# Feed-forward weight splits on two engines, squares read from PSUM, rows of the sparse stage split earlier, two norms tile by tile

## The reference

```
h = x
h = h + stick_breaking_attention(rms_norm(h, g00), w_qkv, w_o)
h = h + sqrelu_mlp(rms_norm(h, g01), w1, w2)          # relu(x @ w1)**2 @ w2, hidden width 4096
shared = nsa_shared_kv(h, kv_norm, w_kv, ...)         # keys and values of the sparse stage
h = h + nsa_attention(rms_norm(h, g10), w_q, gate_b, w_o, shared)
h = h + sqrelu_mlp(rms_norm(h, g11), w1', w2')
x = rms_norm(h, final_norm)                           # end of block one
h = concat(meta_tokens, x); u = rms_norm(h, g_mix)    # start of block two, 528 rows
... differential attention, grouped attention, gates, 16 experts, a last rms_norm
```

## Time and profile before

| | us |
|---|---|
| median of three runs (lowest, highest) | 2800.43 (2799.55, 2804.32) |
| the profiled execution | 2802.55 |
| its span, first to last instruction | 2800.7 |
| TensorE busy in the span | 2511.8 |
| VectorE, GpSimd, ScalarE busy | 1573.0, 1315.5, 781.7 |
| mean granted clock of TensorE | 0.933 of full |

### The profile page before, as it was taken

The page is one execution under the profiler, slowest core; times in us unless marked ns, Lnnn a source line. Parts: engine busy times, 40 slices in busy tenths (PEclk is TensorE's granted clock), DMA queues, the critical chain, the costliest instruction groups (busy, mean ns, idle before and its releaser), DMA issues.

```text
span 2800.7 us, 36947 instructions
## 1 busy us (share of the span) xinstructions
PE 2511.8 (90%) x13831; PEld 1948.4 (70%) x13831; DVE 1573.0 (56%) x2001; ACT 781.7 (28%) x1563; POOL 1315.5 (47%) x1055
## 2 busy tenths in 40 slices
PE   7999899999978889899999689997999899489996
PEld 5787678877566555677777578886988797444442
DVE  3343478765366555286678356663057642666674
ACT  3443200002021554300000333332045400344442
POOL 7553688875031000687788344433752175311111
PEclk9999999999988777999999799998999999599998
DMA  4111333322231000232231211111311030389997
GB/s 125 52 60 38 98 98 97 97 90 83 68 91 53 1 1 1 61 98 90 89 90 53 63 46 46 46 46 46 90 46 31 24 90 23 132 266 349 349 353 252
DMA packets 267866, 268.49 MB, mean 96 GB/s; under 512 B 13339, under 2 KB 198518, under 8 KB 267750
## 3 DMA queue, kind: packets, MB, share of 16 engines
q1 hardware_dynamic: 262998, 253.91, 28.5%
q0 software_dynamic: 4752, 12.98, 1.8%
HBM read 256.10 MB, written 10.75 MB: 95 GB/s over the span
## 4 chain that ended last, share of the span: by engine, by line
PE 61%; DVE 20%; issue 9%; ACT 4%; DMA 4%; POOL 2%; SPq 0%; POOLq 0%; DVEq 0%; ACTq 0%
PE psum L2459 10%; PE psum L2463 9%; PE psum L2462 9%; DVE hid_hi L2718 5%; DVE hid_sq L2717 5%; PE psum L2151 3%; PE psum L1373 3%; DMA ring_tile<-in_w_up 2%; PE psum L2223 2%; PE psum L1157 2%; PE psum L1211 2%; PE psum L1196 2%; PE psum L2289 2%; PE psum L793 1%; PE psum L795 1%
## 5 line engine op out<-in xcount | busy, mean ns | idle before, releaser
L2459 PE MATMUL psum<-x_hi,w_hi 128*128 128x264 f32 (+1 forms) x1536 | 525.3, 342 | 37.5 <-DVE x_lo L706 22.7
L2462 PE MATMUL psum<-x_lo,w_hi 128*128 128x264 f32 (+1 forms) x1536 | 515.3, 336 | 0.0
L752 POOL TENSOR_TENSOR w_hi<-ring_tile,one 128x256 fp32r<-128x256 f32 (+1 forms) x288 | 239.3, 857 | 518.8 <-PE psum L2463 468.5
L2459 PEld LDWEIGHTS psum<-x_hi,w_hi 128*128 128x128 f32 x1536 | 292.2, 190 | 75.1 <-issue 37.2
L2534 POOL TENSOR_TENSOR w_lo<-ring_tile,w_hi 128x1024 fp32r<-128x1024 f32 x128 | 336.9, 2632 | 10.0
L2463 PE MATMUL psum<-x_hi,ring_tile_lo 128*128 128x264 f32 (+1 forms) x1088 | 339.7, 312 | 0.0
L2462 PEld LDWEIGHTS psum<-x_lo,w_hi 128*128 128x128 f32 x1536 | 292.5, 190 | 29.3 <-issue 1.2
L756 POOL TENSOR_TENSOR ring_tile_lo<-ring_tile,w_hi 128x256 fp32r<-128x256 f32 (+1 forms) x288 | 307.0, 1092 | 8.5
L2532 POOL TENSOR_TENSOR w_hi<-ring_tile,one 128x1024 fp32r<-128x1024 f32 x128 | 252.9, 1976 | 116.4 <-PE psum L2463 84.0
L2459 PE MATMUL psum<-w_hi,hid_hi 128*128 128x512 f32 x512 | 202.9, 396 | 21.1 <-DVE hid_lo L2719 21.1
L2463 PEld LDWEIGHTS psum<-x_hi,ring_tile_lo 128*128 128x128 f32 x1088 | 206.4, 190 | 11.7
(11 more groups left out here) (404 smaller groups left out, 5277.2 us busy)
## 6 DMA issues: line engine op xcount, KB each, us to landing
ring_tile<-in_mlp_w SPq DMA_DIRECT2D x128, 512.0 KB, 3.8
ring_tile<-in_w_gate SPq DMA_DIRECT2D x64, 512.0 KB, 7.3
ring_tile<-in_w_up SPq DMA_DIRECT2D x64, 512.0 KB, 7.0
ring_tile<-in_w_down SPq DMA_DIRECT2D x64, 512.0 KB, 8.3
ring_tile<-in_w_in SPq DMA_DIRECT2D x52, 512.0 KB, 3.8
ring_tile<-in_sb_w_qkv SPq DMA_DIRECT2D x24, 512.0 KB, 3.8
ring_tile<-in_nsa_w_kv SPq DMA_DIRECT2D x12, 512.0 KB, 3.6
ring_tile<-in_sb_w_o SPq DMA_DIRECT2D x8, 512.0 KB, 3.6
```

The lines of the kernel that those rows point to most:

```text
L752: last = pool.tensor_tensor(hi[:, cols], raw[:, cols], one[:, :].broadcast_to([P, D // len(parts)]), ALU.mult)
L2459: upper = pe.matmul(dst, a_hi, b_hi, start=first, stop=False)
L2462: pe.matmul(dst, a_hi, b_lo, start=False, stop=False)
```

## The change

1. **Weights of the feed-forward.** ScalarE makes `w_hi` (`ff_upper`, a copy of 1024 columns), GpSimd only `w_lo` (`ff_lower`), in four pieces of 256 columns. ScalarE's copies stand in its order between the relus; the copy of slot j + 4 comes after the relu of tile j. The first two slots of each feed-forward are split ahead of the norm: ScalarE's copies after the norm's first squares, GpSimd's before its statistics.
2. **Squares.** VectorE makes `hid_sq` and `hid_hi` as max(psum, 0) * relu: one operand from the PSUM bank, one from SBUF. TensorE waits for `ff_hid` of the tile four back before it uses the bank again, where it waited for `ff_relu`.
3. **Sparse stage.** `own_x_dve` and `own_x_act` come before the keys; `x3_lo` is made between the two key branches. The query weights are split in four pieces of 256 columns.
4. **Block end.** `flow2_act`, `flow2_pool`, `flow2_dve` do the norms 5 and 6 tile by tile, interleaved with the last residual additions; the meta rows go first. TensorE transposes before it waits for the constants. The waits for the constants and `ready2_dve` come after the norms. SyncE's wait before the constants counts in the new order of updates and is again for the last residual tile.
5. The scratch tile `junk` has another address, and norm 4 writes its squares to `junk_ff`.

```diff
@@ ff_act
+            def part(f, more):
+                upper(f, 2)
+                upper(f, 3)
                 for j in range(FF_TILES):
                     act.wait_ge(ff_mm, n + 1)
-                    act.wait_ge(ff_hid, n + 1)
+                    act.wait_ge(ff_hid, n + 3)
                     act.activation(relu[:, j % 2, :], bank[j % 4][:, :], ACT.Relu).then_inc(ff_relu, 1)
+                    upper(f, j + SPLITS)
+                for j in range(FF_TILES + SPLITS, FF_SLOTS):
+                    upper(f, j)
+                if more:
+                    upper(f + 1, 0)
+                    upper(f + 1, 1)
@@ ff_pool -> ff_lower
-                    pool.tensor_tensor(hi, raw, one[:, :].broadcast_to([P, D]), ALU.mult).then_inc(split_w_hi, 1)
                     pool.wait_ge(split_w_hi, n + 1)
-                    pool.tensor_tensor(lo, raw, hi.bitcast(F32), ALU.subtract).then_inc(split_w, 1)
+            for c in range(4):
+                cols = slice(D // 4 * c, D // 4 * (c + 1))
+                last = pool.tensor_tensor(lo[:, cols], raw[:, cols], hi[:, cols].bitcast(F32), ALU.subtract)
+            last.then_inc(split_w, 1)
@@ ff_dve
-                    dve_t.inc(dve.tensor_tensor(sq, r, r, ALU.mult))
-                    step(dve, dve.tensor_tensor(hid_hi[:, j, :], r, r, ALU.mult))
+                    dve_t.inc(dve.scalar_tensor_tensor(sq, bank[j % 4][:, :], 0.0, r, ALU.max, ALU.mult))
+                    step(dve, dve.scalar_tensor_tensor(hid_hi[:, j, :], bank[j % 4][:, :], 0.0, r, ALU.max, ALU.mult))
@@ ff_pe
-                    pe.wait_ge(ff_relu, n + 1)
+                    pe.wait_ge(ff_hid, n + 1)
@@ kv_dve
+            own_x_dve(dve)
             for br, n0 in ((0, 4), (1, 8)):
...
+                if br == 0:
+                    own_x_lower_dve(dve, range(KT))
                 take_blocks(br, 0, CMP_KT)
-            own_x_dve(dve)
@@ flow2_act
+            whole(6, QT)
...
+            scaled(QT)
+            for s in range(8):
+                if s < QT:
+                    whole(5, s)
+                if 0 <= s - 1 < QT:
+                    whole(6, s - 1)
+                if 0 <= s - 2 < QT:
+                    scaled(s - 2)
+                if s == 3:
+                    split_x_act(act, 6, QT)
+                if 0 <= s - 4 < QT:
+                    split_x_act(act, 6, s - 4)
@@ flow2_dve
+            residual(0)
+            residual(1)
+            plain(0)
+            residual(2)
+            plain(1)
+            residual(3)
+            plain(2)
+            norm_tile_dve(dve, 6, QT)
+            plain(3)
+            for t in range(QT):
+                norm_tile_dve(dve, 6, t)
+                split_x_dve(dve, 6, t - 1 if t else QT)
+            split_x_dve(dve, 6, QT - 1)
@@ block.tensor
+            for t in (QT, 0, 1, 2, 3):
+                norm_tile_pe(pe, 6, t)
             pe.wait_ge(b2_in, B2_CONST)
-            pe.transpose(bank[7][:, 0:3], head_gain_rows[:, :], ident[0:3, 0:3]).then_inc(rows_T, 1)
-            pe.wait_ge(b2_ready, 1)
-            norm_pe(pe, 6)
+            pe.transpose(bank[3][:, 0:3], head_gain_rows[:, :], ident[0:3, 0:3]).then_inc(rows_T, 1)
+            pe.wait_ge(norm_ev, 2 * (norm_base(6) + T2))
             pe.wait_ge(ff_freed, 2)
             ring.wait(pe, "df", 6)
             pe.wait_ge(split_x, split_base(7))
             for _ in df_parts(pe, 0):
                 pass
+            pe.wait_ge(b2_ready, 1)
```

More of the change, by code:

```diff
@@ L613, in turned_bank @@
         def turned_bank(u, t, c):
[L614 removed]
+            return bank[4 * (u in FLOW or u == 6) + 2 * (place(u, t) % 2) + c]
         def norm_act(act, u, updated=None):
@@ new lines, in ff_weight, with ff_upper, ff_upper_freed @@
+        def ff_weight(eng, m, f, j):
+            return ring.wait(eng, f"ff{m}", j, f), w_hi[:, j % SPLITS, :], w_lo[:, j % SPLITS, :]
+        def ff_upper(act, m, f, j):
+            raw, hi, _ = ff_weight(act, m, f, j)
+            act.activation(hi, raw, ACT.Copy).then_inc(split_w_hi, 1)
+        def ff_upper_freed(act, m, upd, f, j, part):
+            w2_frees = FF_TILES // 2 - 1
+            was = (j - SPLITS) % FF_SLOTS
+            half, k = (was - FF_TILES) // (FF_TILES // 2), (was - FF_TILES) % (FF_TILES // 2)
+            if was < FF_TILES:
+                act.wait_ge(ff_mm, f * FF_TILES + (m * FF_PARTS * FF_TILES + was + 1))
+            elif k < w2_frees:
+                act.wait_ge(ff_w2, f * (2 * w2_frees) + ((m * FF_PARTS + part) * 2 * w2_frees + half * w2_frees + k + 1))
+            else:
+                act.wait_ge(acc_done, f * UPD + (upd + (part - 1) * UPD + (half + 1) * QT))
@@ new lines, in ff_pool_first, with ff_pool @@
+        def ff_pool_first(pool, m):
+            for j in range(2):
+                ff_lower(pool, m, 0, j, False)
+        def ff_pool(pool, m):
+            def part(f, more):
+                for j in range(2, FF_SLOTS):
+                    ff_lower(pool, m, f, j)
+                if more:
+                    for j in range(2):
+                        ff_lower(pool, m, f + 1, j)
+            pool.wait_ge(split_w, m * FF_PARTS * FF_SLOTS + 2)
+            pool.wait_ge(slot_free, RING + ring.begin[f"ff{m}"])
+            pool.sem_inc(slot_free, 2)
+            with loop(pool, FF_PARTS - 1) as f:
+                part(f, True)
+            part(FF_PARTS - 1, False)
@@ L2608, in _, with ff_act, upper, part @@
             ex_down_pe(pe, "ex_last", 12, 0, last, 1, False)
-        def ff_act(act, m):
-            with loop(act, FF_PARTS) as f:
+        def ff_act(act, m, upd):
+            def upper(f, j):
+                ff_upper_freed(act, m, upd, f, j, 0 if j < SPLITS else 1)
+                ff_upper(act, m, f, j)
+            def part(f, more):
+                upper(f, 2)
+                upper(f, 3)
                 for j in range(FF_TILES):
```

171 lines of the change are left out of this document (110 added, 61 removed).

## The result

| | before | after |
|---|---|---|
| median, us (runs; lowest, highest) | 2799.99 (4; 2796.35, 2804.32) | 2733.89 (4; 2728.97, 2741.93) |
| ratio of the times, 95% interval | 1 | 0.9766 [0.9737, 0.9795] |
| the profiled execution | 2802.55 | 2731.13 |
| its span; mean granted clock | 2800.7; 0.933 | 2729.0; 0.940 |

The changed kernel takes 66.1 us less; the forecast was 2736, with a range of 2721 to 2754. A second comparison, of five runs, gives 2732.27 against 2797.63, ratio 0.9772 [0.9752, 0.9793]. The same four views are read as before the change. First the page: busy time, share of the span and number of instructions of each engine.

The account below looks back on a forecast made before the run. VectorE, held by GpSimd's instructions, was taken to keep TensorE waiting. 29 + 4.4 + 18 + 13.3 = 64.7 us off the profiled 2802.55 gave 2737.8, or 2736 for the median 2.1 us lower; range 2721 to 2754.

Parts of the forecast that it names:

- What bounds the kernel: VectorE instructions with two SBUF operands stand until GpSimd's current one ends, those reading PSUM do not; TensorE waits behind them.
- Second halves: Feed-forward: waits for hidden tiles and clock drops go, eight second halves take 43.52 us each; 29 us, bounds 24 and 30.2.
- Starts of the feed-forwards: First weight splits done before the norm's statistics, so TensorE starts some 2.2 us earlier, twice; 4.4 us, bounds 2 and 7.
- Sparse stage: TensorE's wait for `x3_lo` after the compression goes, first query at 810.8 instead of 828.90; 18 us, bounds 15.5 and 18.5.
- Block end: Before block two, TensorE waits for weight loads instead of `x_lo`, starting at 1586.1; 13.3 us, bounds 9 and 16.
- A: Feed-forward: the new handover to ScalarE becomes the bound, each part keeps a gap and clock drop; 2764 us, chance 0.08.
- B: Block end gives little, through later loads or a stalled ScalarE; 4 us won there, 2745 us, chance 0.08.
- C: Feed-forward: VectorE's 128 PSUM reads stop TensorE's writes, costing 88 us; slower, 2823 us, chance 0.02.
- E: Whole kernel: more than the sum, as slow-clock attention stretches fall away or GpSimd's shorter work frees more; 2722 us, chance 0.10.
- D: Feed-forward: VectorE held on PSUM reads too, 4.3 us a tile, pieces alone enough, same time; within the forecast's 0.72.
- The sum: Whole kernel: 64.7 us off the profiled 2802.55, giving 2737.8, median 2736; summed bounds 50.5 and 71.7 us.
- half-clock stretches: Attention stages: half-clock stretches may fall otherwise after the change, some 5 us either way.

Follow-up runs that it names:

- the pieces alone: Kernel before, with only GpSimd's feed-forward `w_hi` and `w_lo` splits cut in four pieces each, squares still from SBUF: 2866.15 us against 2798.72.
- the feed-forward alone: Kernel before plus the changes to feed-forward weights and squares and the moved scratch tile, keys and block end as before: 2767.46 us against 2798.72.
- the squares alone: Kernel before, with only the two squares reading PSUM and the waits for `ff_hid` to match, weights whole on GpSimd: 2768.14 us against 2795.95.
- order-only kernel: Kernel before, with only the `x3` rows moved ahead of and amid the keys, query weights split in one piece: 2781.52 us against 2797.63.
- the kernel without PSUM reads: Changed kernel with squares read from `relu` in SBUF again and `w_lo` in one piece, `w_hi` still on ScalarE: 2738.18 us against 2795.95.

## Why the prediction held, point by point

**What bounds the kernel.** That VectorE with two SBUF operands is held, and one that reads PSUM isn't, was read from two neighbouring instructions and from 80 equal additions. It held in 128 new instructions of a kind that no row had. Of the lock's other side it counted up to 0.7 us a slot for GpSimd, which was enough in the changed kernel. It did not count it where it said that the pieces alone are enough: there a slot took 3.68 + 3.27 us. The Trainium skill (SBUF — State Buffer, Who interferes with whom) says that the order of issue decides who blocks. These rows fit that, since both engines' instructions are longer than when free; which of two was issued first they don't show piece by piece.

**Second halves.** Predicted 29 of at most 30.2, measured 30.2 between the two profiled executions. What was kept back for a remainder of small gaps was not needed. GpSimd's load before was read a little high, 5.3 us a slot; its slots follow each other 5.1 us apart in the first half of the earlier trace rows. The sizes: squares 0.69 and 0.68 us (0.6 to 0.74 was said), `hid_lo` 0.97 (0.7 to 1.2), GpSimd 4 x 0.84 = 3.4 us a slot in a first half (2.8 to 3.5).

**Starts of the feed-forwards.** 4.4 predicted. TensorE's wait for `x_lo` is 3.68 and 3.67 us, where it was 6.7 and 5.84. The waits alone give 3.0 + 2.2 = 5.2 us, the starts of the two stages 2.5 + 2.5 = 5.0. From the feed-forward alone less the squares alone it is 31.3 - 27.8 = 3.5, with an interval of some 5 us on each of the two. All within 2 to 7.

**Sparse stage.** 18 predicted, 17.9 in the trace. The chain it was worked out by is there link by link: the gates at once, the hidden values in the time of the gates, the first query 8.4 us behind (8.2 predicted). The one tight place, a key tile taken late with 1 us of slack, has room: VectorE takes it at 755.06 and the next at 756.73, on TensorE's time. The trace of the order-only kernel shows that the pieces were needed for this: without them the hidden values take 5.5 us longer than the gates.

**Block end.** 13.3 predicted, 12.3 measured, and the reason was the right one: a load ends TensorE's wait. It was 1.0 us late against the forecast of 20.3 us behind the last residual. The loads were not slower than before. The 309 GB/s of the earlier trace rows is the best stretch of before; the next one had 291, as the 287 after:

```profile
1580.00:1584.00 4.00, 0.00 (x0) 0.00 (x0) 0.32 (x2) 2.47 (x6) 1.39 (x2) 0.50 1.20 291
```

Nor did they end later, counted from the last residual. The forecast let TensorE start as the traffic stops, and it starts about a microsecond behind that. The Trainium skill (SBUF — State Buffer, A bandwidth-pool intuition that's wrong) gives 358 GB/s, by which they would have ended some 2 us sooner, an estimate; no load of this stage shows that rate, though the constants ahead of them reached 356 in a stretch of 2 us before the change. The profile page after has it elsewhere: in three slices among the experts, the core moves 354 to 357 GB/s.

```profile
GB/s 127 55 55 47 101 100 93 95 97 92 63 116 39 1 1 1 77 94 99 92 100 32 89 39 47 39 55 55 85 40 24 32 90 18 139 289 355 357 354 251
```

The loads of the block end (1516 to 1531 us) and those among the experts (2550 to 2600) differ in the size of their packets, about 0.5 KB and 2.3 KB, with the queues about equally busy. That this makes the difference in rate was not tested.

```profile
DMA packets 6736, 3.27 MB, mean 218 GB/s; under 512 B 592, under 2 KB 6735, under 8 KB 6735
```
```profile
DMA packets 7749, 17.82 MB, mean 356 GB/s; under 512 B 730, under 2 KB 730, under 8 KB 7749
```

A size that was off: the first weights were to be split in 5.2 us and took 3.67 + 3.09 = 6.8, beside VectorE's `x_lo`. This is again GpSimd's side of the lock, hidden under the loads by 2 us.

**Rivals.** A, the handover, did not happen: no wait for `w_lo` or a relu in the second halves. B did not either: the block end gave 12.3 us and not 4. C, reads of PSUM stopping TensorE: 128 of them, and TensorE still has no gap in a second half. E, more than the sum, came in part, in the profiled execution: 3.8 us behind block two's first matmul. D was wrong in its reason. It said that the squares might be held and the time stay the same "since the pieces alone are enough". The time does stay the same, as the kernel without PSUM reads shows, but not thanks to pieces: it has none. What was enough there is that GpSimd has half of its time free. Pieces without that cost 67 us.

**The sum.** 64.7 predicted, 66.1 measured between medians. By stage the terms are off by 1.2, 0.6, -0.1 and -1.0 us, so their agreement isn't made of large errors that cancel. No term had the 2.1 us that came ahead of the keys and in the attention stage, nor the 3.8 behind block two's first matmul. So the profiled execution, forecast at 2737.8, took 2731.13, 6.7 us less, and that the median came within 2.1 us of 2736 is in part luck. The 5 us either way for half-clock stretches were needed: behind the change they take 5 us of the lead and give them back.

## What to carry to other kernels

Where two engines lock each other out, look for who is in the way and for how long, and change the operand of the waiting one before the size of the other's instructions: here an operand in PSUM freed one engine and cost the other nothing, while smaller pieces cost the other engine a fixed price per piece and let it be held in turn. Before cutting work into pieces, add up the pieces on the engine that gets them and hold the sum against what the consumer needs. When a change brings two remedies for one wait, try each alone: here each would have done, and what the second buys is slack.

## What the runs showed of the hardware

Not expected was how much GpSimd loses by small instructions beside a busy VectorE: one `w_hi` of 1024 columns is 1.90 us, in four pieces 2.32 (at 1529.79 in the changed kernel) where VectorE did little, and 3.68 beside its squares. The surplus of pieces alone is 0.4 us, or 0.14 for each of three more instructions; the rest is waiting.

VectorE's operations with one SBUF operand are held too in some cases: an instruction that multiplies `cmp_u` with a constant took 1.86 us beside a whole GpSimd instruction and 0.29 when free. The Trainium skill (SBUF — State Buffer, Who interferes with whom) has such single-operand instructions among those that can take the pair of SBUF ports that VectorE and GpSimd share; the trace agrees. The rows of the kernel before fit the other direction too: a whole `w_hi`, 1.90 us when free, took 5.75 while VectorE mostly multiplied `x3` with its gain, one SBUF tensor and a factor per row.

```profile
794.53 5.75 POOL L752 TENSOR_TENSOR nw_hi<-ring_tile,one 128x1024 fp32r<-128x1024 f32 x1 [102.12 <-DMA ring_tile<-in_nsa_w_q]
```
```profile
794.96 3.30 DVE L1033 TENSOR_SCALAR x<-x,gains 128x512 f32<-128x512 f32 x8
```

So "two SBUF operands", as the prediction put it, is too narrow; "reads PSUM" is the half of the rule that never failed here.
